# Layer 1's modulation rows spread differently over a two-layer trunk on one core: part of them in layer 0's up projection, fewer in its down projection and in the recurrence

## The reference, cut to what matters

```python
for i in range(2):
    mod = silu(c) @ mod_w[i] + mod_b[i]            # 2048 -> 6 * 2048: "modulation rows"
    sh_m, sc_m, g_m, sh_f, sc_f, g_f = split(mod, 6)
    h = rms_norm(x, norm_g[i, 0]) * (1 + sc_m) + sh_m
    y = fox_attention(h) if i == 0 else rwkv7_time_mix(h)
    x = x + g_m * rms_norm(y, norm_g[i, 1])
    h = rms_norm(x, norm_g[i, 2]) * (1 + sc_f) + sh_f
    u = conv3(h @ w_in) + conv_b;  x1, x2 = split(u, 2)     # 2048 -> 11264
    y = (gelu(x1) * x2) @ w_out                             # 5632 -> 2048
    x = x + g_f * rms_norm(y, norm_g[i, 3])
```

## Time and profile before

| | us |
|---|---|
| median of 3 runs | 3105.2 |
| lowest and highest of them | 3092.17 and 3108.06 |
| the profiled execution | 3088.12 |
| its span, first to last instruction | 3086.3 |
| TensorE busy in the span | 2819.0 (91%) |
| VectorE busy | 2048.9 (66%) |
| ScalarE busy | 1465.5 (47%) |
| read from HBM | 623.50 MB, 203 GB/s |

### The profile page before, as it was taken

One profiled execution on the slowest core, in us unless ns is written; L12 is line 12 of the kernel. 1 busy time (PEld: TensorE's weight loads), 2 busy tenths in 40 slices (PEclk: granted clock), 3 DMA queues, 4 the chain that ended last, 5 costly groups with the idle time before them and its releaser, 6 DMA issues.

```text
span 3086.3 us, 61825 instructions
## 1 busy us (share of the span) xinstructions
PE 2819.0 (91%) x23950; PEld 2571.2 (83%) x23950; DVE 2048.9 (66%) x2648; ACT 1465.5 (47%) x2004; POOL 141.7 (5%) x160
## 2 busy tenths in 40 slices
PE   2299999899999999994999899998889999999998
PEld 2299999888888899994888788787878888889998
DVE  6878877877666666668655445544686666666555
ACT  0134343466666643337654332332346666664343
POOL 0000000100000000000000131230000000000000
PEclk8599999999999999996999999999899999999999
DMA  8788888756566668881555432323656665666775
GB/s 290 258 282 302 288 286 297 262 166 192 184 192 187 190 218 294 282 295 51 179 182 174 145 98 94 119 81 98 252 212 197 186 188 180 187 189 212 239 240 170
DMA packets 497960, 628.01 MB, mean 203 GB/s; under 512 B 26392, under 2 KB 434824, under 8 KB 497544
## 3 DMA queue, kind: packets, MB, share of 16 engines
q1 hardware_dynamic: 493760, 622.62, 62.1%
q10 hardware_dynamic: 4040, 3.07, 0.3%
HBM read 623.50 MB, written 2.10 MB: 203 GB/s over the span
## 4 chain that ended last, share of the span: by engine, by line
PE 80%; DVE 9%; DMA 6%; ACT 3%; issue 2%; ACTq 0%; POOL 0%; SPq 0%; DVEq 0%; POOLq 0%
PE ps L1830 27%; PE ps L1814 23%; PE ps L1833 14%; PE ps L2011 11%; DMA raw<-in_ffn_w_out 5%; DVE macc L1196 3%; DVE wlo L1175 2%; ACT whi L753 1%; PE ps L1856 1%; PE ps L1847 1%; PE ps L2065 1%; DVE mx L1521 1%; PE ps L1919 1%; DMA crow<-in_ffn_conv_b 0%; PE ps L1922 0%
## 5 line engine op out<-in xcount | busy, mean ns | idle before, releaser
L1175 DVE TENSOR_TENSOR wlo<-raw,whi 128x1024 fp32r<-128x1024 f32 x792 | 967.2, 1229 | 611.4 <-ACT whi L753 610.2
L753 ACT ACTIVATE whi<-raw 128x1024 fp32r<-128x1024 f32 x792 | 832.2, 1059 | 927.5 <-PE ps L1833 308.7
L1830 PE MATMUL ps<-xs,whi 128*128 128x512 f32 x3328 | 1169.0, 396 | 18.5 <-DVE xs L1259 10.8
L1833 PE MATMUL ps<-xs,wlo 128*128 128x256 f32 x3328 | 935.4, 281 | 0.0
L1830 PEld LDWEIGHTS ps<-xs,whi 128*128 128x128 f32 x3328 | 626.4, 188 | 165.3 <-issue 11.6
L1814 PE MATMUL ps<-act,whi 128*128 128x256 f32 x3840 | 707.6, 287 | 31.4 <-DVE wlo L1175 31.0
L1814 PEld LDWEIGHTS ps<-act,whi 128*128 128x128 f32 x3840 | 607.7, 195 | 37.5 <-DVE wlo L1175 36.8
L1833 PEld LDWEIGHTS ps<-xs,wlo 128*128 128x128 f32 x3328 | 631.6, 190 | 0.0
L1814 PE MATMUL ps<-act,wlo 128*128 128x256 f32 x1920 | 548.4, 286 | 0.0
L1814 PEld LDWEIGHTS ps<-act,wlo 128*128 128x128 f32 x1920 | 373.8, 195 | 0.0
L1196 DVE SCALAR_TENSOR_TENSOR macc<-raw,cact,macc 128x1024 f32<-128x1024 f32 (+1 forms) x308 | 368.2, 1195 | 7.2 <-DMA raw<-in_mod_w 1.8
(11 more groups left out here) (264 smaller groups left out, 2997.1 us busy)
## 6 DMA issues: line engine op xcount, KB each, us to landing
raw<-in_ffn_w_in SPq DMA_DIRECT2D x352, 512.0 KB, 3.7
raw<-in_mod_w SPq DMA_DIRECT2D x288, 512.0 KB, 5.0
raw<-in_ffn_w_out SPq DMA_DIRECT2D x176, 512.0 KB, 4.7
raw<-in_fox_w_in SPq DMA_DIRECT2D x96, 512.0 KB, 5.7
raw<-in_mod_w SPq DMA_DIRECT2D x128, 384.0 KB, 4.8
raw<-in_fox_w_out SPq DMA_DIRECT2D x32, 512.0 KB, 7.3
raw<-in_rwkv_w_r SPq DMA_DIRECT2D x32, 512.0 KB, 4.3
raw<-in_rwkv_w_k SPq DMA_DIRECT2D x32, 512.0 KB, 3.6
```

The source lines that it names most:

```text
L753: sc.activation(whi[:, half, :, :].rearrange("p k n -> p (k n)"), slots[slot], ACT.Copy).then_inc(w_hi, 1)
L1175: v.tensor_tensor(wlo[:, half, :, :].rearrange("p k n -> p (k n)"), slots[slot], whi[:, half, :, :].rearrange("p k n -> p (k n)").bitcast( ...
L1830: pe.matmul(ps[bank + m][:, :], whi[:, half, k, m * P:m * P + P], src[:, kt, :, :].rearrange("p u s -> p (u s)"), start=kt == 0, stop=Fals ...
L1833: last = pe.matmul(ps[bank + m][:, 0:S], wlo[:, half, k, m * P:m * P + P], src[:, kt, 0, :], start=False, stop=kt == KT - 1, skip_group_ch ...
```

## The change

- Up projection 0 runs in six groups of three laps, and four single laps. A group's pattern has 24 `W` and 16 `M` of 768 columns, so each group yields six tiles: 36 in all. The `M` lie between the pieces 5 and 21 of a group (at most one after a piece, none after piece 13). TensorE runs `adaln_sum` at the end of the group, VectorE `adaln_out` after weight piece 4 of the next lap.
- Ring 1 (`raw2`) moves to the end of the `act` buffer; the up projection writes that part only from lap 18 on, past the groups. `macc_up` and `mfin_up` are new, since `ub` and `vb` lie over `macc` and `mfin`; other small tiles share their place later.
- Down projection 0 has 16 instead of 32 `m` a lap: 16 tiles, the same pattern as down projection 1. It writes tiles 32 to 47, and the up projection tiles 0 to 35, so four tiles are worked out twice.
- The recurrence has 256 instead of 512 columns a lap: two tiles, 16 in all. Four pieces of four blocks take the place of eight of two.
- In each out and down lap ScalarE runs a square root of one column ahead of its last `result`. `early(following, 0)` comes behind the root and the residual with the three others. `omu` is computed after down projection 0.

```diff
+UP_GROUP, UP_GROUPS = 3, 6
...
-    ph_up[0] = Phase(UP_ITERS, "W" * 8, early=4)
-    ph_down[0] = Phase(2, "WWWW" + spread(4 * DOWN_PIECES - 4, 2 * KT), early=4)
+    ph_up[0] = Phase(UP_GROUPS, "WWWW" + spread(UP_GROUP * 8 - 6, KT, "M") + "WW", early=4)
+    ph_up_rest = Phase(UP_ITERS - UP_GROUPS * UP_GROUP, "W" * 8)
+    ph_down[0] = Phase(2, "WWWW" + spread(4 * DOWN_PIECES - 4, KT), early=4)
...
-    ph_chunk = Phase(8, "m" * (KT // 2), gemv=1)
+    ph_chunk = Phase(8, "m" * (KT // 4), gemv=1)
...
+        macc_up = take(small, "macc_up", [P, 768])
+        sqsum, _ = at("sqsum", o_sum_up, [P, 2 * S])
...
+        mfin_up = take(small, "mfin_up", [P, 768])
...
-        raw2 = take(r, "raw2", [P, NR, 1024])
+        raw2, _ = at("raw2", O_SMALL - NR * 4096, [P, NR, 1024])
...
+        def up_laps(engine, n, body):
+
+            def grouped(j):
+                for s in range(UP_GROUP):
+                    body(j * UP_GROUP + s, at_start(j, s), ph_up[0], j, 8 * s)
+
+            if n:
+                body(0, True, ph_up[1], 0, 0)
+                with engine.Fori(1, UP_ITERS) as i:
+                    body(i, False, ph_up[1], i, 0)
+                return
+            grouped(0)
+            with engine.Fori(1, UP_GROUPS) as j:
+                grouped(j)
+            past = UP_GROUPS * UP_GROUP
+            body(past, False, ph_up_rest, 0, 0)
+            with engine.Fori(1, UP_ITERS - past) as i:
+                body(i + past, False, ph_up_rest, i, 0)
...
-                for k in range(KT // 2):
+                for k in range(KT // 4):
                     slot = ph_chunk.raw(k)
-                    if not at_start(i, k - NR + 1):
-                        sp.wait_ge(gemv_used, i * (KT // 4) + ((k - NR) // 2 + 1))
-                    sp.dma_start(slots[slot].rearrange("p (k n) -> p k n", k=2),
-                                 mod_w[1][:, 2 * k:2 * k + 2, ds(i * 512 + 32 * P, 512)]).then_inc(raw_in[slot], 16)
+                    if not at_start(i, 0):
+                        sp.wait_ge(gemv_used, i * (KT // 4) + (k - NR + 1))
+                    sp.dma_start(slots[slot].rearrange("p (k n) -> p k n", k=4),
+                                 mod_w[1][:, 4 * k:4 * k + 4, ds(i * 256 + 48 * P, 256)]).then_inc(raw_in[slot], 16)
...
+                    sc.activation(rtab[:, :], eps[0], ACT.Sqrt)
                     result(i, 3)
...
-                early(following, 0)
                 sc.wait_ge(*o["pe"].at("sum"))
...
-                early(following, 1, 2, 3)
+                early(following, 0, 1, 2, 3)
...
-                        sc.activation(mfin[:, 0:512], ps[7][:, :], ACT.Copy).then_inc(gemv_out, 1)
+                        sc.activation(mfin[:, 0:256], ps[7][:, 0:256], ACT.Copy).then_inc(gemv_out, 1)
...
+                    if ph is ph_up[0] and n == 0 and w0 == 0 and not first:
+                        hooks[4] = lambda: adaln_out(ph_up[0], j - 1)
+                    if ph is ph_up_rest and at_start(j, 0):
+                        hooks[4] = lambda: adaln_out(ph_up[0], UP_GROUPS - 1)
+                    pieces(ph, j, hooks, w0, 8)
...
+                    if n == 0 and ph is ph_up[0] and w0 == 8 * (UP_GROUP - 1):
+                        adaln_sum(ph, j)
...
-                for k in (2 * b, 2 * b + 1):
-                    for e in range(2):
-                        kt = 2 * k + e
-                        g = kt % 4
-                        last = pe.matmul(ps[7][32 * g:32 * g + 32, :], cst[:, kt, :],
-                                         slots[ph_chunk.raw(k)][:, 512 * e:512 * e + 512], start=b == 0, stop=b == 3,
-                                         skip_group_check=True, tile_position=(0, 32 * g))
+                for g in range(4):
+                    last = pe.matmul(ps[7][32 * g:32 * g + 32, 0:256], cst[:, 4 * b + g, :],
+                                     slots[ph_chunk.raw(b)][:, 256 * g:256 * g + 256], start=b == 0, stop=b == 3,
+                                     skip_group_check=True, tile_position=(0, 32 * g))
```

More of the change, by code:

```diff
@@ L276, in trunk @@
         ncol = take(small, "ncol", [P, KT])
-        hka = take(small, "hka", [P, KT])
-        hw0 = take(small, "hw0", [P, 2, KT])
-        omu = take(small, "omu", [P, 6 * KT])
         pcol = take(small, "pcol", [P, 4, 2])
@@ L372, in trunk @@
         ysb = take(r3, "ysb", U)
-        pend = [take(small, f"pend{q}", [P, 2, CH]) for q in range(2)]
+        r = [o_sum_up + 8 * S, o_sum_up + 4 * 768]
+        pend = [take(r, f"pend{q}", [P, 2, CH]) for q in range(2)]
+        hka = take(r, "hka", [P, KT])
+        hw0 = take(r, "hw0", [P, 2, KT])
+        omu = take(r, "omu", [P, 6 * KT])
         st = take(r1, "st", [P, 2, 2, HD])
@@ L922, in up_proj @@
             def up_proj(n):
[L924 removed]
+                s = up[n]
                 def side(i, half):
[L928 removed]
+                    sc.wait_ge(w_used, up_weight(n, i, 4 * half + 3))
                     sc.activation(ub[:, 2 * half:2 * half + 2, 2:S + 2], duo[half][:, :, S:2 * S],
@@ L1183, in adaln @@
                 u, kt = divmod(m, KT)
+                part, full = sums(ph)
                 v.wait_ge(raw_in[slot], ph.landed(i, k))
@@ L1189, in adaln @@
                         v.wait_ge(raw_done, ph.done(i, k - 1))
-                    v.tensor_scalar(macc[:, 0:cols], slots[slot][:, 0:cols], cact[:, 0:1], None,
+                    v.tensor_scalar(part[:, 0:cols], slots[slot][:, 0:cols], cact[:, 0:1], None,
                                     ALU.mult).then_inc(raw_done, 1)
@@ L1195, in adaln @@
                     v.wait_ge(mod_summed, ph.unit(i, u - 1))
-                v.scalar_tensor_tensor(mfin[:, 0:cols] if kt == KT - 1 else macc[:, 0:cols], slots[slot][:, 0:cols],
-                                       cact[:, kt:kt + 1], macc[:, 0:cols], ALU.mult, ALU.add).then_inc(raw_done, 1)
+                v.scalar_tensor_tensor(full[:, 0:cols] if kt == KT - 1 else part[:, 0:cols], slots[slot][:, 0:cols],
+                                       cact[:, kt:kt + 1], part[:, 0:cols], ALU.mult, ALU.add).then_inc(raw_done, 1)
             def adaln_out(ph, i, u=0):
@@ L1321, in columns @@
                     *se_v.inc("ncol"))
-                v.tensor_scalar(omu[:, :], col[:, C_MU:C_MU + 6 * KT], -1.0, 1.0, ALU.mult, ALU.add).then_inc(
-                    *se_v.inc("omu"))
             def x_in_tiles(g):
@@ L1509, in _ @@
             out_proj(1, ph_down[0], ph_lora)
+            v.tensor_scalar(omu[:, :], col[:, C_MU:C_MU + 6 * KT], -1.0, 1.0, ALU.mult, ALU.add).then_inc(
+                *mix_zero.inc("omu"))
             x_root(2)
@@ L1845, in adaln_sum @@
                 n = unit_cols[ph] // P
+                full = sums(ph)[1]
                 for t in range(n):
-                    last = pe.matmul(pmod[:, t:t + 1], mfin[:, t * P:t * P + P], ones[:, 0:1], start=True, stop=True,
+                    last = pe.matmul(pmod[:, t:t + 1], full[:, t * P:t * P + P], ones[:, 0:1], start=True, stop=True,
                                      skip_group_check=True)
```

89 lines of the change are left out of this document (52 added, 37 removed).

## The result

| | before | after |
|---|---|---|
| median of 13 runs, us | 3091.8 | 3062.8 |
| lowest and highest, us | 3078.8 and 3108.1 | 3051.1 and 3076.0 |
| profiled execution, us | 3088.1 | 3057.9 |

The ratio of after to before is 0.990, 95% interval 0.988 to 0.992: 31 us faster, 24 to 37 by the interval. The sign and the likeliest case are as predicted.

A forecast was written before the change was run, and what follows sets the result against it. TensorE was taken to bound up projection 0 and the recurrence, a shared four-slot ring down projection 0. Terms -15.8 - 17.9 + 8.9 - 0.1 = -24.9 us took the median from 3105.2 to 3080, range 3066 to 3104.

The forecast's parts named there:

- the likeliest case: Whole kernel: faster, given 0.60, against 0.29 for the same and 0.11 for slower.
- The twin: Down projection 0 would match down projection 1, 260.4 us instead of 276.2, saving 15.8 us.
- The `gemv` step: Recurrence: half the columns save 0.5 us of each 1.0 us call, 2.0 us a lap.
- The copy's 0.2: Recurrence: the `gemv_result` copy behind the fourth call, 0.60 us, falls to 0.385, 0.2 us saved a lap.
- the wait that swallows the sum's half: Recurrence: halving `adaln_sum` (0.98 us) saves 0, as the saving goes into TensorE's 0.59 us wait behind it.
- the 45.8 that I had named as a sign: Recurrence: laps go from 48 to 45.8 us; clearly shorter would mean the halved `adaln_sum` does count.
- The lag of 3.5 us inside a lead of 5.9: Up projection 0 groups: VectorE's lag peaks near 3.5 us, inside its 5.9 us lead, so it costs 0.
- Landings (1): Ring 0 in up projection 0's groups: landings above 7.6 us make weights late; 3131 us at 9 us; 11%.
- VectorE (2): Up projection 0: VectorE becomes the bound in the groups, 70.5 us a group, +16, 3096 us; 10%.
- the clock (3): Up projection 0: the clock drops to half after the six sums, +15 at most, 3095 us; 8%.
- the halved `gemv` (4): Recurrence: it saves nothing, a matmul having a fixed price; +17, 3097 us; 8%.
- pages (5): Up projection 0: instruction pages fetched at each of five group turns, +28 at most, 3094 to 3108 us; 3%.

The follow-up runs named there:

- the run with one column: Kernel after with one matmul instead of two in each adaln_sum of the recurrence; 3069.3 us, one run.
- the first experiment: Kernel after with four modulation tiles per recurrence lap again (512 columns); 3088.1 us (12 runs), ratio to before 0.996.
- the kernel with the old tails: Kernel after without the early square root, the next stage's first piece converted ahead of the root again; 3071.3 us, one run.
- the first eight experiments: Kernel after with one edit each, to recurrence, down projection 0, up projection 0's groups or ring, tails, or doubled tiles; 3052.5 to 3113.4 us.
- that with the late sum: Kernel after with six one-column matmuls put in after lap 10 of up projection 1; 3057.3 us, one run.

## Why the prediction was wrong, and where it was right

**The step that failed is the last one: "so as a median I give 3105.2 - 24.9 = 3080".** Thirteen runs of before have a median of 3091.8, and 23, 20 and 17 others beside the experiments 3096.0, 3096.4 and 3096.0, so 3105.2, the median of three, was 9 to 13 us high. That is 13 of the 17 us by which 3080 missed 3062.8; from 3091.8 the same sum gives 3066.9, just inside the range. The other 4 us are the sum's own: the medians moved by 29.0 and not 24.9. That the sum put on the profiled execution, 3063.2, comes so near the median of 3062.8 is luck: that execution was itself 4 us under the median of before, and its counterpart took 3057.9. That it lay below all three runs was a sign that runs of this kernel scatter by nearly as much as the difference that I forecast, and the right use of it was a range that begins at 3063.2 less the terms' lower bounds (4.1 in the recurrence, 1.5 for the stalls, 0.4 in the tails), 3057. Part of the scatter has a cause that the trace shows, and that is probably the two paces below.

**The sum** of -24.9 us, 0.8%, lies inside the interval of the ratio (0.8 to 1.2%), near its small end. In the profiles it lacks 5.4 us: 3.9 in the recurrence and 9.3 in up projection 1, less 4.8 in the r, k, v projections and 3 elsewhere. The 9.3 us are luck, since before drew the long pace there and after the short one.

**Down projection 0** (forecast -15.8): -14.8 in the profile and 16.0 by undoing the part. The twin was the right row, and the shared ring the cause: with twice the `m` back in it the waits for transfers came back, 154.4 us.

**Recurrence** (forecast -17.9): -21.8, and 22 between the kernels with four tiles and those with two. The `gemv` step was over-sized, 0.43 us a call and not 0.5, since a call has a fixed share. The copy's 0.2 was right (0.22), and so was the wait that swallows the sum's half: it grew by 0.45. The lap in TensorE's own work is 1.94 us shorter, not 2.2. What I didn't look for is the rest, 6 us: laps of before that differ among themselves (47.4 to 48.4) already show that something other than a fixed chain costs time there, and the earlier trace rows are one lap only, 0.5 us longer than the shortest. So a lap of 45.45, under the 45.8 that I had named as a sign that the halved sum counts, was no such sign; the run with one column shows that the sum doesn't count.

**Up projection 0** (forecast +8.9, of which +7.4 for the sums and 1.5 for stalls): +8.0. A sum costs 1.34 us and not 1.23, and there were no stalls. VectorE's share in the groups is 87%, not 92%. A modulation piece has a duration of 1.01 us, but in the dense stretch the next instruction starts 0.93 us after it. VectorE's timeline of after there:

```profile
718.96 1.01 DVE L1244 SCALAR_TENSOR_TENSOR macc_up<-raw,cact,macc_up 128x768 f32<-128x768 f32 x1
719.89 1.22 DVE L1222 TENSOR_TENSOR wlo<-raw,whi 128x1024 fp32r<-128x1024 f32 x1
721.03 0.69 DVE L1510 TENSOR_TENSOR ub<-ps,ub 128x512 f32<-128x512 f32 x1
```

So these queued instructions overlap by some 0.08 us each, and durations added up overstate a busy engine. The lag of 3.5 us inside a lead of 5.9 held as far as TensorE's empty list of waits can show it; the lag itself wasn't measured (and with 0.7 for each `joined` and for the product's low part my own working gives 4.1 and not 3.5). What it rested on, adding up piece by piece and not by the mean, is right, and for the two-lap groups I used the mean and came out low. ScalarE loses more than I had said: 42 table loads of before in the stage have become one. It was not the bound.

**Tails** (forecast -0.1): 0, as far as a profile shows.

**The rivals.** Landings (1) were 4.7 us, far from 7.6; VectorE (2) didn't bound, with 21.3 of 22.2 us in its fullest lap; the clock (3) was 1.00 over all five groups, and behind no sum did it fall; the halved `gemv` (4) saved 86% of what I gave it; pages (5): five turns of the group loop (768 matmuls and weight loads a turn) and not one wait of TensorE, which agrees with the sentence of the Trainium skill ("Runtime: NRT & Kernel Launch", Instruction fetch mechanics) that TensorE's memory holds 2048 instructions, and not with a stall at each taken branch out of two pages. (In the recurrence, which is written out, some waits of TensorE do look like waits for pages, as the first experiment says.) Rivals 1 and 2 are real all the same: two laps to a group bring them both.

## What to carry to other kernels

Make the sum against the execution that the durations come from, and don't take a median of three runs for the kernel's (it was 13 us off here); when the runs of a kernel scatter by more than the effect, first ask the trace for stages of one code that take different times. Before moving work into a stage with room, look at who frees the buffers: the same pieces cost 8 us, all of it their sums, in a ring of their own and 53 us more in the weights' ring. And look at the fullest lap, not at the mean share: two kernels with VectorE at 86 and 87% differ by 50 us. In a chain of small steps read several laps, not one, since part of the cost of fuller laps is in waits and in a lower clock that no single row shows.

## What was not expected

**Two paces of TensorE at one granted clock.** In up projection 1 a lap takes 22.19 or 22.61 us, whatever the kernel, and keeps to it through the stage (but for its first lap and one with a sum). L1883 there in after, and L1884, the same matmul, in the kernel with the old tails:

```profile
L1883 PE MATMUL ps<-xs,whi x1408: 391/391/766, 2281.1 to 2770.3; 128*128 128x512 f32 x176
```

```profile
L1884 PE MATMUL ps<-xs,whi x1408: 395/398/763, 2284.0 to 2782.6; 128*128 128x512 f32 x176
```

The pair of a 512-column and a 256-column matmul is issued every 0.347 or every 0.353 us (22.19 and 22.61 divided by 64). No engine waits more in the one than in the other, and the clock is 1.00 in both, so neither a transfer nor the throttle explains it. Over a stage it is 9.3 us, a third of the whole change. Of the twelve profiles without six such matmuls behind the stage's first lap (before, after, the first eight experiments, that with one matmul, and that with the late sum) five had the long pace in up projection 1.

What the runs say of a cause: the pace is there from the first lap of a stage on, and in nothing but a small sum was it seen to change. Up projection 0 began long in nine of the fourteen profiles, and behind the first sum of twelve matmul records (six one-column matmuls) it was short in all nine; seven of them are free of other waits, and one of the seven is the kernel before with six such matmuls put in. The five stages of up projection 1 that began long had no such sum and stayed long to the end, one of them behind a single one-column matmul; four of them also pass from a written-out first lap into the loop, so that passage doesn't end the pace. A short pace never turned long. That such a sum ends the long pace is therefore well supported, though no run put one in the middle of a long stage of up projection 1: the three profiles with one in that stage had the short pace ahead of it. Why a sum should do so is open, and so is what draws the pace at a stage's start. If it holds, part of what the change gained came unasked, since its sums hold up projection 0 at the short pace from the fourth lap on. How often before has the long pace there wasn't measured: of two profiles with its code up to that place, one began short and one long.

**Half clock where TensorE is busy.** In the recurrence the granted clock fell to half for 3.4 us at a time with TensorE recorded as busy (6.00 of 6.00 us in one window above): inside the laps three times and once in two of the three profiles with four tiles, never in the third or in the laps with two, and once in the laps with none. Each time TensorE had stood idle shortly before, for 1.08 us (1.97 in the laps with none), from some 3 us ahead of the fall on. But it stands idle about as long in every lap, mostly with no fall behind it. So what sets the dips is open.
